# Delta units of a two-block kernel: the order of sends, fetches and copies around unit 0

## The reference, cut to what matters

```python
def gated_deltanet(q, k, v, z, a, b, conv_w, a_log, dt_bias, norm_g):
    ...
    m = jnp.where(strict, bc[..., None] * kk * decay, 0.0)
    lhs = m + jnp.eye(CHUNK, dtype=f32)
    ...
    sol = lax.linalg.triangular_solve(lhs, rhs, left_side=True, lower=True, unit_diagonal=True)
    u, w = sol[..., :A_DV], sol[..., A_DV:]
    ...
    def step(S, inp):
        v_new = u_c - jnp.einsum('bhcd,bhde->bhce', w_c, S)
        o = (jnp.einsum('bhcd,bhde->bhce', q_c * jnp.exp(g_c)[..., None], S)
             + jnp.einsum('bhcs,bhse->bhce', qk_c, v_new))
        S = (S * jnp.exp(g_last)[..., None, None] + jnp.einsum(...))
        return S, o
    ...
    o = rms_norm(o, norm_g) * jax.nn.silu(z.reshape(Bsz, T, A_HEADS, A_DV).astype(f32))
```

## Time and profile before

| what | before |
| --- | --- |
| median of three runs | 2902.95 us |
| the profiled execution, its time | 2902.32 us |
| its span, first to last instruction | 2900.4 us |
| TensorE busy | 2848.9 us, 98% |
| VectorE, ScalarE, GpSimd busy | 51%, 34%, 47% |
| chain that ended last, share of TensorE | 89% |
| mean granted clock of TensorE | 0.995 of 2.4 GHz |

### The profile page before, as it was taken

How to read it: one execution, slowest core, us unless ns; L and a number is a source line. 1 busy time by engine, 2 the same in 40 slices (tenths; PEclk the granted TensorE clock), 3 DMA queues, 4 the chain that set the end, 5 groups by cost and what they waited for, 6 DMA issues and landing times.

```text
span 2900.4 us, 43843 instructions
## 1 busy us (share of the span) xinstructions
PE 2848.9 (98%) x17590; PEld 2502.9 (86%) x17590; DVE 1470.0 (51%) x2412; ACT 986.2 (34%) x1470; POOL 1369.5 (47%) x1748
## 2 busy tenths in 40 slices
PE   9999999999999999999899999999999999999999
PEld 6778888877888888888799999999988799999887
DVE  6955422267532227996445544234897545444241
ACT  3344222255322224333434322223343434322221
POOL 5416554555655555442215555456543214555554
PEclk9989999999999999999999999999999999999999
DMA  5203333322332334223414233232322423322332
GB/s 172 71 23 95 102 90 96 98 95 80 95 99 90 94 99 126 96 67 91 111 52 147 81 94 89 94 90 93 111 73 66 112 81 104 106 95 95 95 93 75
DMA packets 124622, 271.09 MB, mean 93 GB/s; under 512 B 22808, under 2 KB 59032, under 8 KB 124184
## 3 DMA queue, kind: packets, MB, share of 16 engines
q1 hardware_dynamic: 73104, 246.05, 26.8%
q10 hardware_dynamic: 51336, 22.41, 2.9%
HBM read 250.35 MB, written 18.07 MB: 93 GB/s over the span
## 4 chain that ended last, share of the span: by engine, by line
PE 89%; DVE 7%; ACT 2%; issue 1%; ACTq 1%; DMA 0%; POOL 0%; DVEq 0%; POOLq 0%
PE acc L657 67%; PE acc L1054 4%; PE aux L1068 4%; PE acc L706 3%; PE acc L1035 2%; PE aux L1035 2%; PE acc L690 1%; PE aux L874 1%; DVE conv_out L2071 1%; PE aux L939 1%; PE acc L1068 1%; PE acc L1266 1%; PE acc L765 0%; PE aux L829 0%; PE aux L921 0%
## 5 line engine op out<-in xcount | busy, mean ns | idle before, releaser
L629 POOL TENSOR_TENSOR w_lo<-w_raw,w_hi 128x256 fp32r<-128x256 f32 x1744 | 1369.3, 817 | 1514.9 <-ACT w_hi L1300 1514.2
L657 PE MATMUL acc<-n_hi,w_hi 128*128 128x264 f32 (+1 forms) x2832 | 762.0, 324 | 5.5 <-POOL w_lo L629 4.2
L657 PE MATMUL acc<-n_lo,w_hi 128*128 128x264 f32 (+1 forms) x2832 | 752.8, 321 | 0.0
L657 PE MATMUL acc<-n_hi,w_lo 128*128 128x264 f32 (+1 forms) x2832 | 750.8, 320 | 0.0
L1300 ACT ACTIVATE w_hi<-w_raw 128x1024 fp32r<-128x1024 f32 (+1 forms) x436 | 454.8, 1044 | 674.4 <-PE acc L657 605.9
L657 PEld LDWEIGHTS acc<-n_hi,w_hi 128*128 128x128 f32 x2832 | 472.8, 189 | 65.5 <-issue 16.8
L657 PEld LDWEIGHTS acc<-n_lo,w_hi 128*128 128x128 f32 x2832 | 469.7, 188 | 41.3 <-issue 2.6
L657 PEld LDWEIGHTS acc<-n_hi,w_lo 128*128 128x128 f32 x2832 | 469.5, 189 | 38.6
L2173 DVE TENSOR_TENSOR x<-x,acc 128x512 f32<-128x512 f32 (+1 forms) x144 | 99.7, 693 | 565.7 <-PE acc L657 519.3
L657 PE MATMUL acc<-hidden_lo,w_hi 128*128 128x512 f32 (+1 forms) x1040 | 343.6, 358 | 0.0
L657 PE MATMUL acc<-hidden_hi,w_hi 128*128 128x512 f32 (+1 forms) x1040 | 343.0, 357 | 0.0
(11 more groups left out here) (488 smaller groups left out, 3771.3 us busy)
## 6 DMA issues: line engine op xcount, KB each, us to landing
w_raw<-in_stream SPq DMA_DIRECT2D x420, 512.0 KB, 3.5
unit_blocks<-unit_scratch ACTq DMA_DIRECT2D x30, 256.0 KB, 5.0
w_raw<-in_stream SPq DMA_DIRECT2D x16, 384.0 KB, 3.0
unit_scratch<-unit_staged ACTq DMA_DIRECT2D x20, 256.0 KB, 2.6
saved_x<-x SPq DMA_DIRECT2D x2, 2112.0 KB, 8.3
x<-saved_x SPq DMA_DIRECT2D x16, 264.0 KB, 2.7
saved_gates<-root ACTq DMA_DIRECT2D x12, 264.0 KB, 2.1
unit_scratch<-unit_staged ACTq DMA_DIRECT2D x1, 2560.0 KB, 14.6
```

The costliest lines, as they stand in the source:

```text
L629: i = pool.tensor_tensor(wl[:, slot, s], raw[:, slot, s], wh[:, slot, s].bitcast(F32), ALU.subtract)
L657: last = pe.matmul(o, w[:, p % W_SLOTS, P * b:P * b + P], r, start=(b == 0 and i == 0), stop=(b == n - 1 and i == 2))
```

## The change

It has six parts.

- `VALUE_FILL` and `FILL`: one block of z0 moves ahead of the last product of attention; in slot 0 six blocks of z1 stand before the turned tokens and two behind them (before: eight and none).
- `send_solved` sends Y of unit 0 first, on a semaphore of its own (`first_solved_sent`), and no X of unit 0. ScalarE waits for this send, fetches Y of unit 0 and its qk tile, then waits for the other two sends and fetches unit 1. M and X of unit 0 are not fetched.
- In slot 0 ScalarE copies the values first; its weight split follows. The SiLU of z0 and z1, with the second split between them, move to slot 1 behind the first `half`. The five sigmoids of the gate move to slot 5, behind `new_values`.
- `fetch_unit` of the next unit is issued behind the copies of the values in slot u, and no longer for the unit after next at the end of the slot.
- VectorE's `copy_out` comes before the first join of the slot.
- VectorE's `out_mean` comes behind the last subtraction from Y.

```diff
--- before.py
+++ after.py
@@ -60,11 +60,11 @@
 ATTN_FILLERS += [("gate1", 7), ("z", 0)]
 UNIT_FILLERS = [("z", 1), ("gate2", 5), ("z", 2), ("gate2", 6), ("z", 3), ("gate2", 7)]
 FILLERS = ATTN_FILLERS + UNIT_FILLERS
-FILL = [[8, 0, 0, 0, 0, 0, 0]] + [[1, 1, 1, 2, 1, 1, 1]] * 4 + [[2, 1, 2, 0, 0, 0, 3]]
+FILL = [[6, 2, 0, 0, 0, 0, 0]] + [[1, 1, 1, 2, 1, 1, 1]] * 4 + [[2, 1, 2, 0, 0, 0, 3]]
 SCORE_FILL = [[1, 2, 1, 0], [2, 2, 2, 2], [3, 2, 1, 0], [2, 2, 2, 2]]
 TAKEN_BEFORE = [3, 4, 3, 4]
 EARLY, NEXT_UNIT = {2: 3}, (1, 2, 4)
-VALUE_FILL = [[3, 3, 2], [3, 2, 2, 1], [2, 2, 2, 1, 1], [2, 2, 1, 1, 1, 1]]
+VALUE_FILL = [[3, 3, 2], [3, 2, 2, 1], [2, 2, 2, 1, 1], [2, 2, 1, 1, 2, 0]]
 TURN_BANKS = (2, 0)
 TAIL = 24 + TOP_GATES + len(FILLERS)
 BRANCHES = TAIL + KEPT
@@ -487,7 +487,7 @@
     scratch_zero, scratch_clear = sem("scratch_zero_ready"), sem("scratch_clear")
     unit_sent = [sem(f"unit_sent_{n}") for n in range(2)]
     blocks_landed = sem("blocks_landed")
-    blocks_solved, solved_sent = sem("blocks_solved"), sem("solved_sent")
+    blocks_solved, solved_sent, first_sent = sem("blocks_solved"), sem("solved_sent"), sem("first_solved_sent")
     mxy_landed = [sem(f"unit_blocks_landed_{n}") for n in range(2)]
     qkt_landed = [sem(f"qk_t_landed_{n}") for n in range(2)]
     utok_full, utok_ready, vb_ready = sem("tokens_full"), sem("tokens_scaled"), sem("v_tokens_copied")
@@ -1120,7 +1120,7 @@
             else:
                 pe.wait_ge(utok_ready, c.next(utok_ready))
                 pe.wait_ge(vb_ready, c.next(vb_ready, A_HEADS))
-                pe.wait_ge(mxy_landed[0], c.next(mxy_landed[0], 48))
+                pe.wait_ge(mxy_landed[0], c.next(mxy_landed[0], 16))
             mm = heads(acc[:, 2 + u % 2, :], lambda o, h: pe.matmul(o, y_in[:, h, :], vb[:, h, :], start=h == 0, stop=True,
                                                                     skip_group_check=True))
             if u == 0:
@@ -1793,8 +1793,8 @@
 
         def send_solved():
             act.wait_ge(blocks_solved, c.next(blocks_solved))
+            act.dma_start(small_blocks(Y_PART, 0), turned[0:A_HEADS, 1, :, :]).then_inc(first_sent, 16)
             for part, t in ((X_PART, solved), (Y_PART, turned)):
-                act.dma_start(small_blocks(part, 0), t[0:A_HEADS, 1, :, :]).then_inc(solved_sent, 16)
                 act.dma_start(small_blocks(part, 1), t[:, 0, :, :]).then_inc(solved_sent, 16)
 
         def fetch_unit(u, parts=(M_PART, X_PART, Y_PART)):
@@ -1823,10 +1823,7 @@
                 act.wait_ge(uv_full, c.next(uv_full))
                 act.activation(vn[:, :, :], by_head(acc[:, 2 + v % 2, :]), ACT.Copy).then_inc(uv_ready, c.made(uv_ready))
 
-            if u == 0:
-                z_piece = job()
-            else:
-                gap(0)
+            gap(0)
             if v > 0:
                 new_values(v)
             if u < UNITS:
@@ -1834,13 +1831,21 @@
                 for h in range(A_HEADS):
                     act.activation(vb[:, h, :], aux[:, 2, P * h:P * h + P], ACT.Copy, scale=norms[:, 0, u, 4 + h:5 + h])\
                         .then_inc(vb_ready, c.made(vb_ready))
+            if joined and u + 1 < UNITS:
+                fetch_unit(u + 1)
+            if u == UNITS:
+                for m in range(TOP_GATES - 1, KT):
+                    gate_tile(m, at["piece"] - 1)
             if u == 0:
-                silu_of_z(done[0, 0][1], z_piece)
-                for m in range(TOP_GATES - 1, KT):
-                    gate_tile(m, z_piece - 1)
-            gap(1)
+                job()
+            else:
+                gap(1)
             if joined:
                 half(acc[:, 2 + v % 2, :])
+            if u == 1:
+                silu_of_z(ATTN_FILLERS[7][1], at["piece"] - 1)
+                job()
+                silu_of_z(done[0, 1][1], at["piece"] - 1)
             gap(2)
             gap(3)
             if joined:
@@ -1873,8 +1878,6 @@
                         .then_inc(uw_ready, c.made(uw_ready))
                 else:
                     new_values(0)
-                if u + 2 < UNITS:
-                    fetch_unit(u + 2)
                 if v >= 0:
                     out_roots()
 
@@ -1930,11 +1933,10 @@
                     send(j)
                 if j < 3:
                     filler(*ATTN_FILLERS[2 * j + 1])
-            fetch_unit(0, (M_PART,))
-            act.wait_ge(solved_sent, c.next(solved_sent, 64))
-            fetch_unit(0, (X_PART, Y_PART))
+            act.wait_ge(first_sent, c.next(first_sent, 16))
+            fetch_unit(0, (Y_PART,))
             fetch_qk(0)
-            filler(*ATTN_FILLERS[7])
+            act.wait_ge(solved_sent, c.next(solved_sent, 32))
             fetch_unit(1)
             fetch_qk(1)
 
@@ -2527,7 +2529,7 @@
                         dve.wait_ge(gate_sent, c.at(gate_sent))
                     c.next(gate_sent, 16)
                     if m == 5:
-                        dve.wait_ge(solved_sent, 64 * (l + 1))
+                        dve.wait_ge(solved_sent, 32 * (l + 1))
                 a = full()
                 dve.tensor_tensor(wide(dz[:, m, :] if kind == "z" else rt[:, :]), a, wscale, ALU.mult)\
                     .then_inc(taken, c.made(taken))
@@ -2757,7 +2759,7 @@
                 dve.wait_ge(mxy_landed[u % 2], c.next(mxy_landed[u % 2], 48))
                 join_block(0)
             elif u == 0:
-                c.next(mxy_landed[0], 48)
+                c.next(mxy_landed[0], 16)
             if u < UNITS:
                 dve.wait_ge(utok_full, c.next(utok_full))
                 step(dve.tensor_tensor(kge[:, :, :], by_head(aux[:, 0, :]), per_token(5, u), ALU.mult))
@@ -2776,22 +2778,22 @@
                 join_block(1)
                 join_block(2)
             gap(2)
+            if s >= 2:
+                copy_out(s - 2)
             if joined:
                 written = joined_both()
-            if s >= 2:
-                copy_out(s - 2)
             gap(3)
             gap(4)
             if joined:
                 dve.wait_ge(*written)
                 written = joined_both()
             gap(5)
-            if v >= 0:
-                out_mean(v)
             if joined:
                 dve.wait_ge(uy_full, c.next(uy_full))
                 dve.wait_ge(*written)
                 dve.tensor_tensor(y_in, y_in, by_head(aux[:, 2, :]), ALU.subtract).then_inc(uy_ready, c.made(uy_ready))
+            if v >= 0:
+                out_mean(v)
             gap(6)
             if v >= 0:
                 scaled_out(v)
```

## The result

| what | before | after |
| --- | --- | --- |
| median of five runs each, us | 2901.67 (2899.47 to 2904.56) | 2885.74 (2884.66 to 2887.14) |
| span of the profiled execution, us | 2900.4 | 2885.3 |
| mean granted clock | 0.995 | 0.996 |

The ratio of the times is 0.9945, with a 95% interval of 0.9934 to 0.9955: faster by 0.55%. The two medians are 15.9 us apart; 14.9 were forecast, 2888.0 us, and the range of 2884 to 2896 holds the time.

What follows compares the result with a forecast made beforehand. TensorE, busy 98% of the span, was taken as the bound, so only its 51.5 us of gaps could be won. Gains of 7.4 us in layer 0 and 7.5 in layer 1, together 14.9, from 2902.95 gave 2888.0; range 2884 to 2896.

Steps and rivals of the forecast that it cites:

- Part 1: Last attention product: a z block moved ahead lets the first fill continue sooner; gain 0.84 us a layer.
- rival C: Unit 0: Y lands no sooner than the copies of v end now, gap before w_and_u stays; 2895.6 us; chance 0.10.
- Part 2: Unit 0's sends and fetches: earlier copies of v bring w_and_u(0) forward; gain 2.75 us in layer 0, 2.9 in layer 1.
- rival B: Unit 0: ScalarE's queue is the new wait, taking up to 1.7 us a layer; 2891.5 us; chance 0.12.
- Part 3: v_new(0): with the sigmoids moved away, the gap before step_state(0) goes; gain 2.2 us a layer.
- Part 4: Slot 1: SiLUs of z0 and z1 with the split, 3.6 us, fit 4.74 us of idle time; nothing on the path.
- Rival D: Slots 1 and 5: a table switch costs 2.66 us, more than its row; 1.9 us a layer, 2891.8 us; chance 0.04.
- Part 5: Slots 2 and 3: fetches moved into the next slot no longer hold up the root; gain 1.6 us a layer.
- Rival F: Units 2 to 4: later fetches land late and delay TensorE six times; slower, 2915 us at 24.5 us landing; chance 0.05.
- Part 6: VectorE's order at a slot's end, out_mean behind the subtraction from Y: zero, 0.17 us a slot at most.
- Part 7: Slot 5: five sigmoids and a new table load are covered by 1.2 us of slack before turn_out; costs nothing.
- Rivals A: Whole kernel: the forecast holds as summed, 2888 us, own range 2885 to 2891; chance 0.64.

Runs made afterwards that it cites:

- experiment 1: Kernel before with only the last block of z0 moved ahead of the last attention product: 2899.72 us, ratio 0.9995.
- experiment 5: Changed kernel with slot 5's weight split ahead of the square root and its table load: 2884.42 us, ratio 0.9942.
- experiment 6: Changed kernel with the five sigmoids in slot 2, behind the second copy of p, instead of slot 5: 2885.7 us, ratio 0.9948.
- experiment 9: Changed kernel with VectorE's old order in every slot (join ahead of copy_out, out_mean ahead of the last subtraction from Y): 2886.89 us, ratio 0.9946.
- experiment 4: Changed kernel with ScalarE's old order of SiLUs, splits and sigmoids at unit 0, new sends kept: 2891.35 us, ratio 0.9967.
- experiment 3: Changed kernel with the old sends and fetches of unit 0 and one wait for all four sends: 2893.04 us, ratio 0.9977.
- Experiment 2: Kernel before with only the next unit's three fetches moved behind the copies of the values: 2898.35 us, ratio 0.9988.

## Why the prediction was right

| step, us a layer | forecast | measured, layer 0 and 1 |
| --- | --- | --- |
| 1 fill ahead of the product | 0.84 | 0.86, 0.85 |
| 2 w_and_u(0) earlier | 2.75, 2.9 | 2.98, 2.33 |
| 3 w_and_u to step_state | 2.2 | 2.22, 2.22 |
| 5 fetches, slots 2 and 3 | 1.6 | 1.69 |
| 4, 6 slot 1, VectorE's order | 0 | 0 |
| 7 slot 5 | 0 | -0.40, -0.38 |
| sum | 7.4, 7.5 | 7.45, 6.79 by the stretches |

**Part 1** holds to 0.02 us, but as a step of a chain: alone it shows no gain (experiment 1), and the prediction, which gave it 0.84, did not say so. In layer 1 it can hardly have helped even in the whole change: w_and_u has 1.03 us of idle time left there, more than the 0.86, so by these rows it would have begun at the same time without the move (an estimate, no run has the change without it). Only the sum of parts 1 and 2 is a measured gain. In rival C I let it stand while the gap before w_and_u stayed; by experiment 1 that was not to be expected.

**Part 2.** The mechanism is as written: Y lands in time, since w_and_u begins 0.10 us after the copies of v end and not later, and ScalarE's queue frees these copies. The wait of 0.55 us came out as 0.18 and 1.03. The term was taken for both layers from the issues of layer 0. Y's issue took 1.87 (2.07 forecast), the last four 2.14 in layer 0 (2.4 forecast) but 3.26 in layer 1. So rival B is there, in one layer, with 0.6 us against the forecast, a third of the 1.7 a layer it had been given. That it is not the tile is shown by experiments 5, 6 and 9, where its issue takes 0.53 and the fetches ahead of it the rest. The sign "w_and_u(0) within 1 us of the end of its fill" was missed in layer 1 by 0.03.

**Part 3** is right in size and cause (experiment 4). Removed with the gaps was the half clock of layer 1. It gave nothing of its own there, since v_new and not TensorE set the 5.52 us. What neither the prediction nor the expectation of experiment 3 priced is what that clock costs once v_new is early: the experiment was to cost 3 to 5 us and cost 8.4.

**Part 4.** The block was forecast at 3.6 us in a cover of 4.74, and 1.30 us are left idle. The activation behind the table load starts 0.01 us after its end (1423.78 + 1.28 = 1425.06, the row says 1425.07). Rival D falls with it. The Trainium skill (ScalarE: Activation LUTs, What ACT_TABLE_LOAD costs) gives 1283 ns for the load, which the 1.28 us here bear out, and 1380 ns for a drain, which these rows have neither ahead of the load nor behind it.

**Part 5.** 0.83 in slot 2 and 0.86 in slot 3 (2.60 us from 1462.02 to 1464.62). Experiment 2 has the same two distances with the fetches moved alone. The 0.15 taken back for copy_out was not needed: experiment 9. Rival F's late landing is not there. In VectorE's list of waits after the change (total us, times, longest), the joins wait for a fetch twice, once a layer, and both waits are unit 1's:

```profile
DVE unit_a L2748 <- DMA unit_blocks<-unit_scratch: 4.4, 2, 2.6
```

Before it was 6.3 us in two. Units 2 to 4, whose fetches were moved, have none.

**Part 6** is zero within 0.1 us, by experiment 9, which undoes it together with the move of copy_out.

**Part 7 failed.** I had followed the new table load to the root, to scaled_out and to turn_out, and there it is covered: turn_out has no idle time. What I left out is what is queued behind the root on ScalarE: the split, and behind the split GpSimd. "Nothing" measured 0.4 us a layer. The split ends 1.08 us later relative to turn_out (2.69 less 1.61), GpSimd's low parts run beside all four of VectorE's products with z, these take 0.67 us more, of which 0.28 comes back in the low parts behind them, and VectorE's eviction behind those is what the branch product waits for. Experiments 5 and 6 remove the loss in two ways, 5 with the table load still in place. VectorE's eviction from PSUM beside GpSimd keeps its 0.69 us (1520.06). What is stretched reads two tensors of SBUF: the products (1238 ns against 780) and the low parts behind them (1237 ns in the median, against 696 for the next four, when GpSimd is done). The Trainium skill (GPSIMD Engine Reference, 1. Specifications) says that GpSimd shares its SBUF interfaces with VectorE and contends with VectorE's instructions that have two SBUF inputs; the rows agree, with these numbers.

Rivals A and B describe what happened; C, D, E and F did not come. The time came out 2.3 us under the forecast. 1.3 of that is the starting point: 2902.95 was the median of three runs, and with five it is 2901.67. The other 1.0, by which the medians went beyond the sum, is not evidence for any step: by the stretches the change gave 14.24 us, 0.7 less than the 14.9 forecast (0.8 in part 7, 0.6 in part 2 of layer 1, less some tenths won elsewhere), and 0.97 us of the spans' difference arose at the program's start. That the two medians differ by almost the forecast has some luck in it: the losses in part 7 and in layer 1, which the prediction did not price, stand beside differences of the same size that the change does not touch.

## What to carry to other kernels

Behind a chain of small steps, ask of each edit what it waits for next: a block moved ahead of one wait won 0.86 us there, and with the next wait in place no gain of it was left to see. When an instruction is added to an engine, follow what is queued behind it to the other engines as well, not only to the result for whose sake it is there: here the split behind the root, and GpSimd behind the split. Transfers that nobody reads can cost more than their bytes where they sit in the queue of an engine that has something else to do.

## What the runs showed of the hardware

- How long a DMA's issue holds ScalarE is not a property of the transfer. The same fetch of unit 1's qk tile took 0.66 us in layer 0 and 1.78 in layer 1, 1.59 in layer 0 of experiment 1, and 0.53 in layer 1 of experiments 5, 6 and 9, where the three fetches ahead took 2.61 to 2.83 us instead of 1.48.
- In experiment 3 the granted clock was 0.50 behind gaps of 2.31 and 2.92 us, in experiment 1 behind 5.15. It was 1.00 in experiment 4, layer 0, behind gaps of 1.19 and 2.04, and in experiment 2 a gap of 2.06 had 0.50 behind it in layer 0. In the kernel before it stayed at 1.00 through a gap of 3.16 us in layer 0 and fell behind one of 3.34 in layer 1. The length of a gap alone does not tell.
- VectorE's product of two SBUF tensors, 128x528 in fp32, took 754 ns at the least and 1238 with GpSimd's subtraction beside it. GpSimd is slowed as well: in the changed kernel, layer 0, its instructions took 752 ns in the median before VectorE's products (1512.5 to 1515.5 us) and 1199 beside them (to 1520).
